# Value panels of the gated feed-forward by seven block products as well

## The chip, the cores and the metric

The kernel runs on one core of a Trainium2 chip. It is one program that does everything from the inputs in the chip's memory to the stored output. The metric is the device time of the launch in microseconds (us). Before the change it is 2545.13 us, the median of three runs (2545.09 to 2545.74).

## The reference

Two transformer blocks of two layers each run over one sequence of 512 tokens with 1024 features. The change touches only the gated feed-forward, which ends both layers of the second block:

```
def swiglu(h, w_in, w_out):
    gu = h @ w_in                       # 1024 x 5632
    gate, up = jnp.split(gu, 2, axis=-1)
    return (jax.nn.silu(gate) * up) @ w_out     # 2816 x 1024
...
x = x + g2 * swiglu(h, ffn_w_in[i], ffn_w_out[i])
```

Everything is in 32-bit floats. The kernel gets that accuracy out of matmuls on rounded numbers: each operand is split into a high part and the rest (low), and a product is low x high, high x low and high x high, three matmuls added up in PSUM.

## The kernel before, in words

**Panels.** Weights come in panels of 128 partitions x 2048 numbers (1 MB). Panel number `at` lies in buffer `at % 2` of three tiles: `RAW` (as loaded), `WH` (high part) and `WL` (low part). SyncE loads a panel into `RAW` as soon as the panel two before it has been split (`split_done`), in the order of the panels. GpSimd (POOL) splits a panel once TensorE has begun the panel before it (`panels_begun`), since only then are `WH` and `WL` of that buffer free. TensorE may begin a panel when it is split.

**One feed-forward** has 11 chunks of 256 hidden features. A chunk has three panels: a gate panel, a value panel (1024 x 256 each) and a down panel (256 x 1024). TensorE's order is: gate of chunk c+1, value of chunk c+1, down of chunk c, gate of chunk c+2, and so on. I call these the stages G, V and D. In D, eight output tiles i = 0..7 go into the banks `DOWN_BANKS`; VectorE (DVE) adds each to the residual `X` (`add`, `residual`, line 3040 of the profile). TensorE waits before tile i for the count of adds `DOWN_FREE[i]`: tile 7 waits until tiles 0 to 3 of this D have been added (bank 1 is used twice).

**Seven block products (`up_fast`).** From chunk 2 on (`FAST_FROM`) the gate panel is multiplied as a 2 x 2 block product with seven half-width products in place of eight (Strassen-Winograd). Each product is 4 x 3 matmuls of 256 columns, 84 in all, where `hidden_t` takes 2 x 8 x 3 = 48 matmuls of 512 columns. The sums that this needs are made beside it:
- `weight_sums`, four DVE operations of 128x512 from `RAW` into `w_sums` (steps 0 to 3); ScalarE (ACT) copies them rounded to `w_sums_hi` (`sums_high`), GpSimd makes `w_sums_lo` (first half of `split_fast`, four operations) and then the low part of the panel (three operations, since one quarter isn't needed); the panel's high part is made by ScalarE (`panel_high`);
- `copy_first` (ACT) copies product 1 within PSUM, and TensorE's product 3 adds to it; `copies` (ACT) take products 2 and 5 out; `combine_first` and `combine` (DVE, four operations of 128x256) add them up. TensorE waits for `copy_first` before product 3 and for `combine_first` before product 5.
- Gate's `up_fast` begins when tiles 0 to 4 of the D before it have been added, and its `copy_first` writes bank 1, so it waits for all eight.

The value panel goes by `hidden_t`, and both it and the down panel are split by GpSimd alone (`split_pieces`: one operation for the high part, four for the low).

**The hidden features** of a chunk: `Silu` of the gate (ACT), times the value (DVE, `u_in`), high part `U` (ACT, `uhi`), low part (DVE, `ulo`), used by the D of the chunk one round later. Each engine's order is written out by hand in its own `swiglu` and `chunk`; within an engine nothing overtakes. DVE's round is: combine the gate, weight sums of the next gate, value times silu, low part, eight adds. The loop takes two chunks a turn; the semaphore counts go by `number`, `fast_at` and `loads`.

Of the kernel before, what the change touches and what calls it, by code (L numbers as in the profile page):

```python
# [26 lines left out]
ALU = mybir.AluOpType  # L27
# [5 lines left out]
KT = D // P  # L33
# [18 lines left out]
DIL = 4  # L52
D_FF2 = 2816
FF2_CHUNKS = D_FF2 // 256
FAST = (0,)
FAST_FROM = 2
FAST_PANELS = len(FAST) * (FF2_CHUNKS - FAST_FROM)
PARTS = 16 * LAYERS + 20
# [10 lines left out]
PN_A = LAYERS * PN_LAYER  # L69
# [364 lines left out]
def build(nc, t, out):  # L434
    with ExitStack() as ctx:
# [478 lines left out]
        def _(pool):  # L914
# [30 lines left out]
            def split_pieces(at):  # L945

                b = at % 2
                pool.wait_ge(raw_ready[b], 16 * loads(at))
                pool.wait_ge(s.panels_begun, at + 2)
                apart(pool)  # L950
                pool.tensor_scalar(WH[b][:, :], RAW[b][:, :], 1.0, 1.0, ALU.mult, ALU.mult).then_inc(s.split_hi, 1)  # L951
                pool.wait_ge(s.split_hi, at + 1)
                for q in range(4):
                    c = slice(S * q, S * q + S)
                    ins = pool.tensor_tensor(WL[b][:, c], RAW[b][:, c], WH[b][:, c].bitcast(F32), ALU.subtract)  # L955
                ins.then_inc(s.split_done, 1)
# [1436 lines left out]
        def _(act):  # L2393
# [388 lines left out]
            def swiglu(w, first, g0, f0, u0):  # L2782

                def number(z, c):

                    return (c - FAST_FROM) * len(FAST) + (FAST_PANELS * w + FAST.index(z))

                def copy_first(z, c):

                    n = number(z, c)  # L2790
                    act.wait_ge(fa.products, fa.products_0 + (n * 5 + 1))
                    if z == 0:
                        act.wait_ge(s.f_evac, c * 8 + (f0 + BANKS - 8))
                    f(PS[:, 3 * z + 1, 0:256], PS[:, 3 * z, 0:256], ACT.Copy).then_inc(fa.copied, 1)

                def copies(z, c):

                    n = number(z, c)
                    act.wait_ge(fa.products, fa.products_0 + (n * 5 + 2))
                    f(p5_copy(z), PS[:, 3 * z + 2, 0:256], ACT.Copy).then_inc(fa.copied, 1)  # L2800
                    act.wait_ge(fa.products, fa.products_0 + (n * 5 + 4))
                    f(p167_copy(z), PS[:, 3 * z + 1, 0:256], ACT.Copy).then_inc(fa.copied, 1)

                def panel_high(z, c, b):

                    act.wait_ge(s.panels_begun, c * 3 + (first + 1 + z))
                    f(WH[b][:, :], RAW[b][:, :], ACT.Copy).then_inc(s.split_hi, 1)

                def sums_high(z, c):

                    if z in FAST:
                        act.wait_ge(fa.sums, fa.sums_0 + ((c - FAST_FROM) * len(FAST) * 4 + ((FAST_PANELS * w + FAST.index(z) + 1) * 4 + 9 * (w + 1))))
                        f(w_sums_hi(z), w_sums(z), ACT.Copy).then_inc(fa.sums_hi, 1)  # L2813

                def chunk(c, e, fast, ahead, normed=False):

                    b0 = (first + e) % 2
                    gate_fast, value_fast = (fast and z in FAST for z in range(2))
                    if value_fast:
                        panel_high(1, c, b0)  # L2820
                    if gate_fast:
                        copy_first(0, c)
                        copies(0, c)
                        act.wait_ge(fa.combined, fa.combined_0 + (number(0, c) * 4 + 4))
                    if value_fast:
                        copy_first(1, c)
                    halves = range(2) if gate_fast else range(1)
                    for j in range(2):
                        act.wait_ge(s.g_tile, c * 4 + (g0 + j + 1))
                        for h in halves:  # L2830
                            src = quarter(0, True, j, h) if gate_fast else PS[:, j, :]
                            dst = SQ[:, j, 256 * h:256 * h + 256] if gate_fast else SQ[:, j, :]
                            ins = f(dst, src, ACT.Silu)
                        ins.then_inc(s.r32, 1)
                    if normed:
                        for x in range(4):
                            act.wait_ge(fa.sums, fa.sums_0 + ((FAST_PANELS * 4 + 9) * w + x + 2))
                            f(h_sums_hi(x), h_sums(x), ACT.Copy).then_inc(fa.sums_hi, 1)
                    if value_fast:
                        copies(1, c)  # L2840
                    if ahead:
                        sums_high(0, c + 1)
                        panel_high(0, c + 1, b0)
                    for j in range(2):
                        if value_fast:
                            act.wait_ge(s.u_in, c * 2 + (u0 + 2))
                            for h in range(2):
                                ins = f(U[:, e, j, 0, 256 * h:256 * h + 256], quarter(1, True, j, h), ACT.Copy)
                            if j:
                                ins.then_inc(s.uhi, 2)  # L2850
                        else:
                            act.wait_ge(s.u_in, c * 2 + (u0 + j + 1))
                            f(U[:, e, j, 0, :], PS[:, 3 + j, :], ACT.Copy).then_inc(s.uhi, 1)
                    if ahead:
                        sums_high(1, c + 1)

                chunk(0, 0, False, False, normed=True)
                chunk(1, 1, False, True)
                with act.Fori(0, (FF2_CHUNKS - 3) // 2) as c2:
                    for e in range(2):  # L2860
                        chunk(c2 * 2 + (2 + e), e, True, True)
                chunk(FF2_CHUNKS - 1, 0, True, False)

            enter(act, ST_A)
            act.dma_start(near, t["dist"][:, D_A:D_A + 3 * P]).then_inc(s.dist_in, 16)
# [132 lines left out]
        def _(dve):  # L2998
# [433 lines left out]
            def swiglu(w, first, g0, f0, u0, gate, norm, add_last=None):  # L3432

                def number(z, c):

                    return (c - FAST_FROM) * len(FAST) + (FAST_PANELS * w + FAST.index(z))
# [56 lines left out]
                        v.wait_ge(fa.sums_hi, fa.sums_hi_0 + ((FAST_PANELS + 4) * w + x + 1))  # L3493
                        v.tensor_tensor(h_sums_lo(x), h_sums(x), h_sums_hi(x).bitcast(F32), ALU.subtract).then_inc(fa.sums, 1)

                def hidden(c, e, fast, ahead=None):

                    gate_fast, value_fast = (fast and z in FAST for z in range(2))
                    if gate_fast:
                        combine_first(0, c)  # L3500
                        combine(0, c)
                    if ahead:
                        weight_sums(0, c + 1, *ahead[0], range(2))
                    if value_fast:
                        combine_first(1, c)
                    if ahead:
                        weight_sums(0, c + 1, *ahead[0], range(2, 4))
                    if value_fast:
                        combine(1, c)
                        v.wait_ge(fa.combined, fa.combined_0 + (number(1, c) * 4 + 4))  # L3510
                    halves = range(2) if value_fast else range(1)
                    for j in range(2):
                        v.wait_ge(s.r32, c * 2 + (u0 - 64 + j + 1))
                        v.wait_ge(s.g_tile, c * 4 + (g0 + 2 + j + 1))
                        for h in halves:
                            x = quarter(1, True, j, h) if len(halves) == 2 else PS[:, 3 + j, :]
                            y = SQ[:, j, 256 * h:256 * h + 256] if len(halves) == 2 else SQ[:, j, :]
                            ins = v.tensor_tensor(x, y, x, ALU.mult)
                        if len(halves) == 1 or j:
                            ins.then_inc(s.u_in, len(halves))  # L3520
                    for j in range(2):
                        v.wait_ge(s.uhi, c * 2 + (u0 + (2 if len(halves) == 2 else j + 1)))
                        for h in halves:
                            x = quarter(1, True, j, h) if len(halves) == 2 else PS[:, 3 + j, :]
                            hi, lo = (U[:, e, j, y, 256 * h:256 * h + 256] if len(halves) == 2 else U[:, e, j, y, :] for y in range(2))
                            ins = v.tensor_tensor(lo, x, hi.bitcast(F32), ALU.subtract)
                        ins.then_inc(s.ulo, 1)
# [4 lines left out]

                def chunk(c, e, fast, ahead):

                    hidden(c + 1, e, fast, ahead)
                    for i in range(4):
                        add(c, range(i, i + 1))
                        if ahead:
                            weight_sums(1, c + 2, *ahead[1], range(i, i + 1))
                    add(c, range(4, KT))  # L3540

                def panel_loaded(c, z, c2=None):

# [163 lines left out]
```

## Time and profile before

| | |
|---|---|
| runs | 2545.09, 2545.13, 2545.74 us |
| profiled execution | 2544.84 us, its span 2543.1 us |
| TensorE | busy 2514.6 us (99%), granted clock 0.999 |
| DVE, ACT, GpSimd | busy 52%, 30%, 56% |
| one round (G, V, D) of the gated feed-forward | 31.86 us |

The span runs from the first instruction to the last; 1.74 us lie around it. Matmuls are pipelined, so that the start of one to the start of the next counts (the pitch), not the duration of one.

### The profile page before, as it was taken

How to read it: one execution, taken by the hardware profiler on the slowest of the kernel's cores; microseconds unless marked ns; L12 is line 12 of the kernel's file. 1: busy time of each engine (PE TensorE's matmuls, PEld its weight loads, DVE VectorE, ACT ScalarE, POOL GpSimd, SP SyncE). 2: the span in 40 equal slices, each digit the busy share in tenths (PEclk: the TensorE clock that was granted, in tenths of full speed). 3: DMA queues.
4: the chain of work that ended last, by engine and by line, in shares of the span. 5: the costliest groups of instructions: out<-in, count | busy, mean ns of one | idle time of the engine just before them, and what ended most of it. 6: DMA issues, size and time to landing. Idle time of an engine off the chain costs nothing. (4 is left out here: it accounts for less than half of the span.)

```text
span 2543.1 us, 37266 instructions
## 1 busy us (share of the span) xinstructions
PE 2514.6 (99%) x15183; PEld 2062.2 (81%) x15183; DVE 1321.6 (52%) x2134; ACT 764.7 (30%) x1483; POOL 1422.2 (56%) x796
## 2 busy tenths in 40 slices
PE   8999999999999999999999999999999999999999
PEld 6787778888887877788888767788888888788888
DVE  4445565666534346656665344655554135755554
ACT  5245451111123454511011443322222333422223
POOL 5543246666565423356655833677776522677776
PEclk9999999999999999999999999999999999999999
DMA  8321034555333211445562211223233211232232
GB/s 268 83 61 51 22 112 149 191 188 185 115 101 83 62 49 34 133 138 181 195 199 100 70 51 36 89 94 99 99 99 126 83 51 35 83 98 99 98 99 71
DMA packets 220459, 265.50 MB, mean 104 GB/s; under 512 B 19236, under 2 KB 192892, under 8 KB 220188
## 3 DMA queue, kind: packets, MB, share of 16 engines
q1 hardware_dynamic: 217628, 256.72, 31.4%
q10 hardware_dynamic: 2688, 6.76, 0.8%
q8 instruction: 104, 1.70, 0.3%
q14 instruction: 39, 0.32, 0.0%
HBM read 258.74 MB, written 4.72 MB: 104 GB/s over the span
## 5 line engine op out<-in xcount | busy, mean ns | idle before, releaser
L923 POOL TENSOR_SCALAR WH<-RAW 128x2048 fp32r<-128x2048 f32 x112 | 215.4, 1924 | 713.3 <-issue 608.7
L925 POOL TENSOR_TENSOR WL<-RAW,WH 128x2048 fp32r<-128x2048 f32 x112 | 519.0, 4634 | 9.3
L1115 PE MATMUL PS<-Hh,WL 128*128 128x512 f32 x864 | 337.3, 390 | 0.7 <-POOL WL L955 0.7
L1118 PE MATMUL PS<-Hl,WH 128*128 128x512 f32 x864 | 336.4, 389 | 0.0
L1119 PE MATMUL PS<-Hh,WH 128*128 128x512 f32 x864 | 336.1, 389 | 0.0
L3040 DVE SCALAR_TENSOR_TENSOR X<-PS,X 128x512 f32<-128x512 f32 x304 | 207.0, 688 | 185.5 <-PE PS L1868 123.3
L955 POOL TENSOR_TENSOR WL<-RAW,WH 128x512 fp32r<-128x512 f32 x192 | 277.7, 1474 | 4.0
L2775 ACT ACTIVATE PS<-SQ 128x512 f32<-128x512 f32 x64 | 38.5, 602 | 557.1 <-DVE SQ L3381 557.1
L1864 PE MATMUL PS<-U,WL 128*128 128x512 f32 x512 | 200.1, 391 | 0.0
L1867 PE MATMUL PS<-U,WH 128*128 128x512 f32 x512 | 199.2, 389 | 0.0
L1868 PE MATMUL PS<-U,WH 128*128 128x512 f32 x512 | 199.2, 389 | 0.0
L1115 PEld LDWEIGHTS PS<-Hh,WL 128*128 128x128 f32 x864 | 162.2, 188 | 35.7 <-POOL WL L955 2.2
L1119 PEld LDWEIGHTS PS<-Hh,WH 128*128 128x128 f32 x864 | 162.2, 188 | 33.9
L1118 PEld LDWEIGHTS PS<-Hl,WH 128*128 128x128 f32 x864 | 162.3, 188 | 32.8
L951 POOL TENSOR_SCALAR WH<-RAW 128x2048 fp32r<-128x2048 f32 x48 | 92.5, 1928 | 162.6 <-issue 162.6
L3040 DVE SCALAR_TENSOR_TENSOR X<-PS,MOD,X 128x512 f32<-128x512 f32 x184 | 132.4, 746 | 64.9 <-PE PS L1986 48.1
L1985 PE MATMUL PS<-U,WH 128*128 128x512 f32 x336 | 130.7, 389 | 0.0
L1986 PE MATMUL PS<-U,WH 128*128 128x512 f32 x336 | 130.7, 389 | 0.0
L1982 PE MATMUL PS<-U,WL 128*128 128x512 f32 x336 | 130.7, 389 | 0.0
L934 POOL TENSOR_TENSOR YL<-DB,YL 128x512 fp32r<-128x512 f32 x72 | 91.0, 1295 | 50.9 <-ACT YL L2813 50.9
L1864 PEld LDWEIGHTS PS<-U,WL 128*128 128x128 f32 x512 | 96.1, 188 | 21.1 <-issue 1.2
L1868 PEld LDWEIGHTS PS<-U,WH 128*128 128x128 f32 x512 | 96.1, 188 | 20.1
(636 smaller groups left out, 5878.6 us busy)
## 6 DMA issues: line engine op xcount, KB each, us to landing
RAW<-in_w_ff SPq DMA_DIRECT2D x64, 1024.0 KB, 5.3
PROJ<-in_ada_w SPq DMA_DIRECT2D x48, 1024.0 KB, 7.9
RAW<-in_ffn_w_in SPq DMA_DIRECT2D x44, 1024.0 KB, 5.1
RAW<-in_ffn_w_out SPq DMA_DIRECT2D x22, 1024.0 KB, 4.9
RAW<-in_w_in SPq DMA_DIRECT2D x20, 1024.0 KB, 5.3
RAW<-in_w_out SPq DMA_DIRECT2D x8, 1024.0 KB, 5.1
RAW<-in_a_w_in SPq DMA_DIRECT2D x6, 1024.0 KB, 5.0
RAW<-in_b_w_in SPq DMA_DIRECT2D x12, 512.0 KB, 5.1
```

What stands on the lines that cost most here:

```text
L923: pool.tensor_scalar(WH[b][:, :], RAW[b][:, :], 1.0, 1.0, ALU.mult, ALU.mult).then_inc(s.split_hi, 1)
L925: pool.tensor_tensor(WL[b][:, :], RAW[b][:, :], WH[b][:, :].bitcast(F32), ALU.subtract).then_inc(s.split_done, 1)
L955: ins = pool.tensor_tensor(WL[b][:, c], RAW[b][:, c], WH[b][:, c].bitcast(F32), ALU.subtract)
L1115: ins = mm(bank, WL[b][:, col:col + P], Hh[:, k, :], start=k == 0, stop=False)
L1118: mm(bank, WH[b][:, col:col + P], Hl[:, k, :], start=False, stop=False)
L1119: ins = mm(bank, WH[b][:, col:col + P], Hh[:, k, :], start=False, stop=k == KT - 1)
L1864: ins = mm(bank, WL[b][:, col:col + P], U[:, c % 2, k, 0, :], start=k == 0, stop=False)
L1867: mm(bank, WH[b][:, col:col + P], U[:, c % 2, k, 1, :], start=False, stop=False)
L1868: ins = mm(bank, WH[b][:, col:col + P], U[:, c % 2, k, 0, :], start=False, stop=k == 1)
L1982: ins = mm(bank, WL[b][:, col:col + P], U[:, e, k, 0, :], start=k == 0, stop=False)
L1985: mm(bank, WH[b][:, col:col + P], U[:, e, k, 1, :], start=False, stop=False)
L3040: v.scalar_tensor_tensor(X[:, tile, :], PS[:, bank, :], gate, X[:, tile, :], ALU.mult, ALU.add).then_inc(evac, 1)
```

## The change

`FAST` becomes `(0, 1)`: the value panels of chunks 2 to 10 go by seven block products as well, 9 in each feed-forward, 18 in all. For them `w_sums` lie in other tiles (`ATT`, `ATTR`, `MEMTR`). With it the order of the helpers moves:
- ACT makes the high part of the value panels (`panel_high(1, ...)`, first thing in G) and of the down panels D(1) to D(9) (`panel_high(2, ...)`, in V ahead of the value's `copy_first`); GpSimd drops that operation in `split_fast` and `split_pieces`. `sums_high(1, ...)` stands before the `U` copies.
- DVE (`hidden`): steps 0 and 1 of the next gate's sums, `combine_first` of the value, steps 2 and 3, `combine` of the value. Then (`between(0)`) the adds of tiles 0 to 3 with the four steps of the next value's sums between them (add 0, steps 0 and 1, add 1, step 2, add 2, step 3, add 3), then value times silu (four of 128x256), adds 4 and 5 (`between(1)`), the low part (four of 128x256), adds 6 and 7.

```diff
--- before.py
+++ after.py
@@ -52,7 +52,7 @@
 DIL = 4
 D_FF2 = 2816
 FF2_CHUNKS = D_FF2 // 256
-FAST = (0,)
+FAST = (0, 1)
 FAST_FROM = 2
 FAST_PANELS = len(FAST) * (FF2_CHUNKS - FAST_FROM)
 PARTS = 16 * LAYERS + 20
@@ -948,7 +948,8 @@
                 pool.wait_ge(raw_ready[b], 16 * loads(at))
                 pool.wait_ge(s.panels_begun, at + 2)
                 apart(pool)
-                pool.tensor_scalar(WH[b][:, :], RAW[b][:, :], 1.0, 1.0, ALU.mult, ALU.mult).then_inc(s.split_hi, 1)
+                if 1 not in FAST or not any(at in range(first + 7, first + 3 * FF2_CHUNKS - 1, 3) for first in (PN_A + 10, PN_B + 11)):
+                    pool.tensor_scalar(WH[b][:, :], RAW[b][:, :], 1.0, 1.0, ALU.mult, ALU.mult).then_inc(s.split_hi, 1)
                 pool.wait_ge(s.split_hi, at + 1)
                 for q in range(4):
                     c = slice(S * q, S * q + S)
@@ -2812,7 +2813,7 @@
                         act.wait_ge(fa.sums, fa.sums_0 + ((c - FAST_FROM) * len(FAST) * 4 + ((FAST_PANELS * w + FAST.index(z) + 1) * 4 + 9 * (w + 1))))
                         f(w_sums_hi(z), w_sums(z), ACT.Copy).then_inc(fa.sums_hi, 1)
 
-                def chunk(c, e, fast, ahead, normed=False):
+                def chunk(c, e, fast, ahead, normed=False, loaded=None):
 
                     b0 = (first + e) % 2
                     gate_fast, value_fast = (fast and z in FAST for z in range(2))
@@ -2823,6 +2824,8 @@
                         copies(0, c)
                         act.wait_ge(fa.combined, fa.combined_0 + (number(0, c) * 4 + 4))
                     if value_fast:
+                        act.wait_ge(raw_ready[1 - b0], loaded)
+                        panel_high(2, c, 1 - b0)
                         copy_first(1, c)
                     halves = range(2) if gate_fast else range(1)
                     for j in range(2):
@@ -2841,6 +2844,7 @@
                     if ahead:
                         sums_high(0, c + 1)
                         panel_high(0, c + 1, b0)
+                        sums_high(1, c + 1)
                     for j in range(2):
                         if value_fast:
                             act.wait_ge(s.u_in, c * 2 + (u0 + 2))
@@ -2851,15 +2855,14 @@
                         else:
                             act.wait_ge(s.u_in, c * 2 + (u0 + j + 1))
                             f(U[:, e, j, 0, :], PS[:, 3 + j, :], ACT.Copy).then_inc(s.uhi, 1)
-                    if ahead:
-                        sums_high(1, c + 1)
-
+
+                down_loads = lambda c: 16 * loads(first + 3 * c + 1)
                 chunk(0, 0, False, False, normed=True)
                 chunk(1, 1, False, True)
                 with act.Fori(0, (FF2_CHUNKS - 3) // 2) as c2:
                     for e in range(2):
-                        chunk(c2 * 2 + (2 + e), e, True, True)
-                chunk(FF2_CHUNKS - 1, 0, True, False)
+                        chunk(c2 * 2 + (2 + e), e, True, True, loaded=c2 * 48 + down_loads(2 + e))
+                chunk(FF2_CHUNKS - 1, 0, True, False, loaded=down_loads(FF2_CHUNKS - 1))
 
             enter(act, ST_A)
             act.dma_start(near, t["dist"][:, D_A:D_A + 3 * P]).then_inc(s.dist_in, 16)
@@ -3493,7 +3496,7 @@
                         v.wait_ge(fa.sums_hi, fa.sums_hi_0 + ((FAST_PANELS + 4) * w + x + 1))
                         v.tensor_tensor(h_sums_lo(x), h_sums(x), h_sums_hi(x).bitcast(F32), ALU.subtract).then_inc(fa.sums, 1)
 
-                def hidden(c, e, fast, ahead=None):
+                def hidden(c, e, fast, ahead=None, between=None):
 
                     gate_fast, value_fast = (fast and z in FAST for z in range(2))
                     if gate_fast:
@@ -3507,6 +3510,9 @@
                         weight_sums(0, c + 1, *ahead[0], range(2, 4))
                     if value_fast:
                         combine(1, c)
+                    if between:
+                        between(0)
+                    if value_fast:
                         v.wait_ge(fa.combined, fa.combined_0 + (number(1, c) * 4 + 4))
                     halves = range(2) if value_fast else range(1)
                     for j in range(2):
@@ -3518,6 +3524,8 @@
                             ins = v.tensor_tensor(x, y, x, ALU.mult)
                         if len(halves) == 1 or j:
                             ins.then_inc(s.u_in, len(halves))
+                    if between:
+                        between(1)
                     for j in range(2):
                         v.wait_ge(s.uhi, c * 2 + (u0 + (2 if len(halves) == 2 else j + 1)))
                         for h in halves:
@@ -3532,12 +3540,18 @@
 
                 def chunk(c, e, fast, ahead):
 
-                    hidden(c + 1, e, fast, ahead)
-                    for i in range(4):
-                        add(c, range(i, i + 1))
-                        if ahead:
-                            weight_sums(1, c + 2, *ahead[1], range(i, i + 1))
-                    add(c, range(4, KT))
+                    def between(x):
+
+                        if x:
+                            add(c, range(4, 6))
+                            return
+                        for i in range(4):
+                            add(c, range(i, i + 1))
+                            if ahead:
+                                weight_sums(1, c + 2, *ahead[1], ((0, 1), (2,), (3,), ())[i])
+
+                    hidden(c + 1, e, fast, ahead, between)
+                    add(c, range(6, KT))
 
                 def panel_loaded(c, z, c2=None):
```

## Rows read from the trace of the kernel before

**Rows 1.** The page, part 1: busy time of TensorE.

```profile
PE 2514.6 (99%) x15183; PEld 2062.2 (81%) x15183; DVE 1321.6 (52%) x2134; ACT 764.7 (30%) x1483; POOL 1422.2 (56%) x796
```

**Rows 2.** Waits of TensorE, 1640 to 1980 us: total, times, longest.

```profile
PE PS L1088 <- ACT Hh L2438: 0.7, 1, 0.7
PE PS L1115 <- POOL WL L955: 0.4, 1, 0.4
```

**Rows 3.** Windows: one round in mid-stage; length, busy time by engine, clock, DMA.

```profile
1759.34:1791.20 31.86, 31.86 (x182) 28.09 (x181) 16.71 (x20) 7.03 (x11) 24.05 (x17) 1.00 0.30 98
```

**Rows 4.** Timeline of TensorE: start, duration; first matmul of G, V, D, G.

```profile
1759.34 0.28 PE L1941 MATMUL PS<-Hh,WL 128*128 128x256 f32 x1
...
1769.41 0.40 PE L1115 MATMUL PS<-Hh,WL 128*128 128x512 f32 x1
...
1780.32 0.39 PE L1982 MATMUL PS<-U,WL 128*128 128x512 f32 x1
...
1791.19 0.28 PE L1941 MATMUL PS<-Hh,WL 128*128 128x256 f32 x1
```

**Rows 5.** Timeline of DVE in that round: start, duration, line, idle before.

```profile
1759.54 0.75 DVE L3040 SCALAR_TENSOR_TENSOR X<-PS,MOD,X 128x512 f32<-128x512 f32 x1 [0.61 <-PE PS L1986]
1763.95 0.42 DVE L3443 TENSOR_TENSOR PTS<-PS,PTS 128x256 f32<-128x256 f32 x1 [3.66 <-PE PS L1945]
...
1769.61 0.43 DVE L3455 TENSOR_TENSOR PS<-RS,PS 128x256 f32<-128x256 f32 x1 [0.92 <-PE PS L1945]
1772.12 1.71 DVE L3467 TENSOR_TENSOR DB<-RAW 128x512 f32<-128x512 f32 x1 [2.08 <-DMA RAW<-in_ffn_w_in]
1773.75 1.77 DVE L3469 TENSOR_TENSOR DB<-RAW 128x512 f32<-128x512 f32 x1
1775.45 1.78 DVE L3472 TENSOR_TENSOR DB<-DB,RAW 128x512 f32<-128x512 f32 x1
...
1784.40 2.72 DVE L3040 SCALAR_TENSOR_TENSOR X<-PS,MOD,X 128x512 f32<-128x512 f32 x4
```

**Rows 6.** Timeline of ACT in that round.

```profile
1761.05 0.37 ACT L2794 ACTIVATE PS<-PS 128x256 f32<-128x256 f32 x1 [9.27 <-PE PS L1945]
...
1770.15 1.21 ACT L2833 ACTIVATE SQ<-PS 128x256 f32<-128x256 f32 x4 [3.04 <-DVE PS L3455]
1778.96 1.92 ACT L2813 ACTIVATE YL<-DB 128x2048 fp32r<-128x2048 f32 x1 [7.59 <-DVE DB L3475]
1780.78 1.90 ACT L2807 ACTIVATE WH<-RAW 128x2048 fp32r<-128x2048 f32 x1
```

**Rows 7.** Timeline of GpSimd in that round.

```profile
1759.80 1.90 POOL L951 TENSOR_SCALAR WH<-RAW 128x2048 fp32r<-128x2048 f32 x1 [1.80 <-issue]
1761.78 5.05 POOL L955 TENSOR_TENSOR WL<-RAW,WH 128x512 fp32r<-128x512 f32 x4
...
1771.99 6.38 POOL L955 TENSOR_TENSOR WL<-RAW,WH 128x512 fp32r<-128x512 f32 x4
1781.05 5.05 POOL L934 TENSOR_TENSOR YL<-DB,YL 128x512 fp32r<-128x512 f32 x4 [2.68 <-ACT YL L2813]
```

**Rows 8.** Timeline of GpSimd in two short windows, where single operations come apart.

```profile
1774.94 3.43 POOL L955 TENSOR_TENSOR WL<-RAW,WH 128x512 fp32r<-128x512 f32 x2
...
1776.64 1.73 POOL L955 TENSOR_TENSOR WL<-RAW,WH 128x512 fp32r<-128x512 f32 x1
```

**Rows 9.** Timeline, ahead of the first D: DVE and then GpSimd.

```profile
1650.51 0.68 DVE L3472 TENSOR_TENSOR DB<-DB,RAW 128x512 f32<-128x512 f32 x1
...
1644.55 5.49 POOL L955 TENSOR_TENSOR WL<-RAW,WH 128x512 fp32r<-128x512 f32 x4
```

**Rows 10.** Timeline of TensorE: first matmul of the first D and of V(2).

```profile
1652.88 0.39 PE L1982 MATMUL PS<-U,WL 128*128 128x512 f32 x1
...
1673.83 0.40 PE L1115 MATMUL PS<-Hh,WL 128*128 128x512 f32 x1
```

**Rows 11.** Timeline, 1024-wide passes: DVE beside GpSimd's splits.

```profile
1623.27 2.32 DVE L3486 TENSOR_TENSOR PROJ<-MEMT,ATT 128x1024 f32<-128x1024 f32 x1
1625.51 2.32 DVE L3488 TENSOR_TENSOR PROJ<-MEMT,PROJ 128x1024 f32<-128x1024 f32 x1
```

## The prediction

> **What bounds the kernel now.** I read the page first: TensorE is busy for 99% of the span [rows 1], so only fewer TensorE cycles or new TensorE idle time can move the end. Then its waits over the nine rounds of the first gated feed-forward: 1.1 us in all, none of it in a fast round [rows 2]. The window of one round says the same: 31.86 us long, TensorE busy for all of it, DVE for 16.71, ACT 7.03, GpSimd 24.05 [rows 3]. TensorE is the bound, with no slack used up; the helpers have room on average. An average doesn't say whether they have it at the right moment, so I laid out one round from the timelines of the four engines [rows 4 to 8].
>
> **The gain.** G is 84 matmuls in 1769.41 - 1759.34 = 10.07 us (pitch 0.120 us), V is 48 in 10.91 us (0.227), D is 48 in 10.87 [rows 4]. Half the columns cost 53% of the time, so seven products in place of eight give little: a fast V should take 10.07, 0.84 less. Times 18 panels: -15.1 us. That is all the change can give.
>
> **Small costs.** GpSimd loses two 1.90 us operations a round [rows 7], gains four of sums_lo (5.05) and drops one low quarter (1.26): it stays at 24 us of about 31. ACT gains three 128x2048 passes of 1.9 and a few small ones: 14 of 31. Their averages are fine; their places matter twice.
> - G: ACT now starts with panel_high(1). It sees G begun 0.46 after the first matmul (as GpSimd at 1759.80 [rows 7]) and takes 1.90, pitch 1.81; copy_first moves from G+1.71 [rows 6] to G+2.27 and ends at +2.64. Product 3's weights load at about G+2.76. I book 0 (bounds 0 and 0.2).
> - V: ACT is held by gate's last combine until V+0.74 (1770.15 [rows 6]); panel_high(2) puts the value's copy_first to 2.55 to 2.92, with product 3 due at 2.88. I book 0.25 a round (bounds 0.1 and 0.5), 4.5 us in all. Silus (pitch 0.27) and product 2's copy follow until V+4.4; combine_first at 4.9 still comes before product 5 wants it at 6.0.
>
> **The price of a weight sum.** A 128x512 sum takes 0.68 us when GpSimd rests [rows 9], and 1.7 us beside GpSimd's low-part operations [rows 5]. The two interlace: GpSimd's operations start at 1774.94 and 1776.64 [rows 8], DVE's at 1773.75 and 1775.45 [rows 5], each pair 1.70 apart. GpSimd's operation alone is 1.26 (5.05 / 4 [rows 7]), so DVE's sum ends some 0.5 after the GpSimd operation that was running, and that engine's next one waits as long. A 1024-wide pass fits: 2.24 from start to start [rows 11], that is 1.26 plus twice the 0.5. DVE's adds, with one input in PSUM, run at 0.66 whether GpSimd is busy or not (2.72 for four [rows 5]). So in a row: a sum ends 0.5 after the current GpSimd operation, and an add between two sums lies under the next GpSimd operation and is nearly free (sum to sum 1.70 to 1.75 with it). The bound on the other side is that it isn't: 1.70 for each sum plus 0.66 for each add.
> The Trainium skill, SBUF — State Buffer, section "SBUF: two separate sides", speaks against this change too: VectorE with two SBUF inputs and GpSimd hold one port pair exclusively, for a whole instruction, and the other blocks. The trace agrees (1.70 against 0.68). By it the adds hide and the sum is the one below; by shared bandwidth it would be the dearer bound.
>
> **The chain that I expect to set the round.** The new value sums can't start before the next value panel is in RAW, and that load waits for the down panel's split in the same buffer, which waits for V to begin. From V's first matmul (0), in the steady state:
> - ACT's panel_high(2) ends at 2.64; GpSimd starts the low part at 2.8 (0.17 later, as from 1780.88 to 1781.05 [rows 6, 7]). Its four operations interlace with three of gate's sums; alone 5.05, so 6.38 as now [rows 7], and DVE's wait for combine_first leaves one gap more: done at 9.35.
> - From there to the first sum: 5.29, as from 1766.83 (1761.78 + 5.05) to 1772.12 [rows 5, 7]. The value's sums start at 14.65. D began at 10.3, tile 0 is long added.
> - GpSimd meanwhile has the next gate panel: sums_high ends at 10.1, so 7 operations from 10.27 (5.05 + 3.8 alone). All four sums meet them: step 0 ends 15.85 (behind GpSimd's fourth), step 1 17.55, add 1 inside, step 2 19.3, step 3 21.0, add 3 21.7.
> - TensorE's tile 7 wants add 3. It was due at 10.3 + 9.5 = 19.8: about 1.9 late. D's last tile ends 23.1.
> - Value times silu: four 256-wide (0.42 each [rows 5], pitch about 0.34): 23.05. Add 4: 23.75; G wants it and starts at 23.9, 0.8 more.
> - Add 5 to 24.4, low part 24.45 to 25.9 (ACT's sums_high(1), 1.9, and U copies end 24.4), adds 6 and 7 to 27.25. Gate's copy_first wants add 7: 27.35 to 27.7; product 3 starts at 27.85 where 26.8 was due: 1.05 more. The other five products take 7.19, and the next V begins at 35.05.
> GpSimd, on the other side, is done with the next value panel at 32.0, and the next gate panel lands at 37.3, 2.25 after V's start, as the layout assumed. The round closes: 35.05 in place of 31.86, +3.2 a round, gain and V's 0.25 included.
>
> **The sum.** Nine rounds from D(0)..D(8) to V(2)..V(10). In the first, D(0) starts at 1652.88 and the panel's split ends at 1650.04 [rows 9, 10]: sums from 1655.3, next V 20.4 later (27.25 - 14.65 + 7.8) at 1675.8 to 1676.3 in place of 1673.83: +2.2. Eight full rounds: 8 x 3.2 = 25.5. The last V: -0.84 + 0.25 = -0.6. Together 27.1, and the second feed-forward alike: +54.2 us. On the profiled execution's 2544.84 us (span 2543.1 and 1.74 around it, 0.3 under the median of 2545.13) that gives 2599.0 us.
>
> **Bounds.** If adds don't hide under GpSimd's operations, three adds cost 0.66 each and the sums begin no earlier: up to 0.95 a round more once the last sum runs partly alone, 2616; with the 256-wide operations at their full 0.43 (0.6 a round over eight, half of it felt) 2622. If two of the four value sums find GpSimd at rest (its seven operations over early), they cost 0.65 for 1.7: about 2 us a round less, +18, 2563. 0.2% (5 us) is about what a measurement of this kernel can tell from no change.
>
> **Rivals.**
> 1. The chain fits and the gain is seen: faster. It needs the value's sums at 0.68 and GpSimd unhindered: the split done at 7.86, sums from 13.15, add 3 at 17.6 with tile 7 due at 19.8, add 7 at about 23.3 with copy_first due at 23.4. The round is then TensorE's 31.02 + 0.25: -15.1 + 4.5 = -10.6, 2534 us. It decides once the chain is under 31.86, 3.2 us shorter than mine. For it: the helpers' averages leave room, and the trace shows sums only beside GpSimd's line 955, where mine meet line 934 too. Against it: the paired starts [rows 5, 8]. 14%.
> 2. The same chain, but DVE pays the full 1.7 for every sum and the adds on top: round 36.0, 2616 us. For it: no row shows an add between two sums. Against: the 1024-wide pass, which splits 2.24 into a wait and its own time. 20%.
> 3. Part of the lateness is absorbed, since a late G gives GpSimd time and it meets fewer sums: a round within 0.3 of 31.86, no measurable change. For it: only the room on average. 4%.
> The forecast as written: 62%. Slower by over 0.2% are the forecast and rival 2, 82%, with rival 3's same at 4% and faster 14%. The range takes in the bounds of the forecast and rival 2, 2563 to 2622; it leaves out rivals 1 and 3 and 2% beyond.
>
> **What the profile after would show.** TensorE's waits: tile 7's first matmul (line 1982 of before) on DVE's add (line 3040), some 1.9 us, 18 times; G's first matmul on the same for 0.8; product 3 of the gate on ACT's copy for 1.0; product 3 of the value for 0.25. Value sums of 1.2 to 1.8 us between the adds, starting some 4.3 after D's first matmul. A round of 35 us, with DVE's idle time gone between there and G. It would be wrong if the sums run at 0.7, if the load comes long before D+4, or if the adds of tiles 0 to 3 end before D+9.5.

## The result: 2594.41 us, 1.9% slower, and the profile after

The changed kernel takes 2594.41 us (median of four runs, 2593.85 to 2596.02), the kernel before 2545.24 on the same chips. The ratio is 1.0194, 95% interval 1.0176 to 1.0212: slower, by 49 us. The forecast was 2599.0 (2563 to 2622). The profiled execution took 2596.02 us with a span of 2594.0, 51.2 above the profiled execution of before; it is the slowest of the four.

The page says first where to look. The row of [rows 1] has become this one, and a TensorE line with idle time in front of it is among the costly groups:

```profile
PE 2520.4 (97%) x15831; PEld 2081.1 (80%) x15831; DVE 1415.1 (55%) x2350; ACT 888.5 (34%) x1627; POOL 1448.9 (56%) x814
...
L1983 PE MATMUL PS<-U,WL 128*128 128x512 f32 x336 | 133.1, 396 | 24.8 <-DVE X L3043 24.8
```

TensorE's share fell from 99% to 97%: it waits. GpSimd's share is the 56% of before, which speaks against its amount of work as the cause (one of the experiments tests it). TensorE's waits over the whole span (total, times, longest), where [rows 2] had nothing:

```profile
PE PS L1983 <- DVE X L3043: 24.8, 18, 1.7
...
PE PS L1942 <- ACT PS L2795: 8.1, 17, 0.7
PE PS L1942 <- DVE X L3043: 8.0, 17, 0.5
```

Line 1983 is the first matmul of a down tile and waits for an add 18 times (tile 7); line 1942 (first matmul of each step of a half-width product) waits for an add at the start of G and for ACT's copy ahead of product 3. The windows of one round, stage by stage (G, V, D; the columns are those of [rows 3]):

```profile
1805.30:1816.19 10.89, 10.43 (x84) 10.23 (x85) 4.42 (x10) 3.34 (x6) 8.04 (x7) 1.00 0.22 78
1816.19:1826.54 10.35, 10.33 (x87) 10.13 (x85) 6.96 (x8) 5.88 (x9) 6.66 (x4) 1.00 0.18 62
1826.54:1840.19 13.65, 11.41 (x51) 8.69 (x49) 10.43 (x15) 4.69 (x6) 10.89 (x8) 1.00 0.40 125
```

V did get shorter, 10.35 for 10.91. D grew from 10.87 to 13.65 and G from 10.07 to 10.89. A round is 34.87 us (278.96 from V(2) to V(10), over 8) in place of 31.86; the first two are longer, 35.14 and 35.32, since TensorE waits there for `combine_first` ahead of the value's product 5 (0.54 and 1.77 us), and the other six are 34.75 on average. DVE's timeline in D and the next G shows why a round is long:

```profile
1830.94 1.28 DVE L3470 TENSOR_TENSOR ATT<-RAW 128x512 f32<-128x512 f32 x1 [2.06 <-DMA RAW<-in_ffn_w_in]
1832.15 1.77 DVE L3472 TENSOR_TENSOR ATT<-RAW 128x512 f32<-128x512 f32 x1
1833.85 0.74 DVE L3043 SCALAR_TENSOR_TENSOR X<-PS,MOD,X 128x512 f32<-128x512 f32 x1
1834.51 1.12 DVE L3475 TENSOR_TENSOR ATT<-ATT,RAW 128x512 f32<-128x512 f32 x1
1835.55 0.74 DVE L3043 SCALAR_TENSOR_TENSOR X<-PS,MOD,X 128x512 f32<-128x512 f32 x1
1836.21 1.10 DVE L3478 TENSOR_TENSOR ATT<-RAW,ATT 128x512 f32<-128x512 f32 x1
1837.24 0.74 DVE L3043 SCALAR_TENSOR_TENSOR X<-PS,MOD,X 128x512 f32<-128x512 f32 x1
1837.90 1.41 DVE L3524 TENSOR_TENSOR PS<-SQ,PS 128x256 f32<-128x256 f32 x4
1839.22 1.40 DVE L3043 SCALAR_TENSOR_TENSOR X<-PS,MOD,X 128x512 f32<-128x512 f32 x2
1840.59 1.42 DVE L3534 TENSOR_TENSOR U<-PS,U 128x256 fp32r<-128x256 f32 x4
1841.93 1.40 DVE L3043 SCALAR_TENSOR_TENSOR X<-PS,MOD,X 128x512 f32<-128x512 f32 x2
```

The row at 1830.94 waits for the load of the next value panel; behind it DVE has not a moment's rest until 1843.33, and the adds that TensorE wants stand in that queue. From one sum to the next, with an add between them, it is 1.70 us (1834.51 to 1836.21), as long as sum to sum without one ([rows 5]). The load waits for GpSimd's split of the down panel, which waits for ACT, and ACT for DVE's last combine of the gate, 0.6 us after V's start at 1816.19:

```profile
1817.01 1.92 ACT L2808 ACTIVATE WH<-RAW 128x2048 fp32r<-128x2048 f32 x1 [3.11 <-DVE PS L3458]
```

```profile
1819.01 6.66 POOL L956 TENSOR_TENSOR WL<-RAW,WH 128x512 fp32r<-128x512 f32 x4 [5.67 <-ACT WH L2808]
```

GpSimd sat idle for 5.67 us before it. And TensorE, in the D and G one round ahead of those rows of DVE, at tile 7 (1803.15), at G (1805.30) and at gate's product 3 (1808.89); a round later the three waits are 1.74, 0.50 and 0.46:

```profile
1803.15 0.50 PE L1983 MATMUL PS<-U,WL 128*128 128x512 f32 x1 [1.60 <-DVE X L3043]
...
1805.30 0.38 PE L1942 MATMUL PS<-Hh,WL 128*128 128x256 f32 x1 [0.50 <-DVE X L3043]
...
1808.89 0.39 PE L1942 MATMUL PS<-PROJR,YL 128*128 128x256 f32 x1 [0.46 <-ACT PS L2795]
```

### The profile page after: what moved, and what is told of

Read it like the earlier page. It is cut to its first block and busy times, and to the rows that moved or that the text cites. A ratio compares the mean times of both kernels' runs of the same rounds, so it can differ in the third digit from the quotient of the medians.

```text
span 2594.0 us, 39234 instructions
## 1 busy us (share of the span) xinstructions
PE 2520.4 (97%) x15831; PEld 2081.1 (80%) x15831; DVE 1415.1 (55%) x2350; ACT 888.5 (34%) x1627; POOL 1448.9 (56%) x814
## 3 DMA queue, kind: packets, MB, share of 16 engines
q8 instruction: 106, 1.74, 0.3%
## 5 line engine op out<-in xcount | busy, mean ns | idle before, releaser
L923 POOL TENSOR_SCALAR WH<-RAW 128x2048 fp32r<-128x2048 f32 x112 | 215.8, 1926 | 713.4 <-issue 594.4
L956 POOL TENSOR_TENSOR WL<-RAW,WH 128x512 fp32r<-128x512 f32 x120 | 188.3, 1599 | 100.7 <-ACT WH L2808 99.7
L1116 PE MATMUL PS<-Hh,WL 128*128 128x512 f32 x576 | 225.0, 391 | 0.8 <-POOL WL L956 0.8
L1119 PE MATMUL PS<-Hl,WH 128*128 128x512 f32 x576 | 224.1, 389 | 0.0
L1120 PE MATMUL PS<-Hh,WH 128*128 128x512 f32 x576 | 224.1, 389 | 0.0
L1116 PEld LDWEIGHTS PS<-Hh,WL 128*128 128x128 f32 x576 | 108.1, 188 | 24.7 <-POOL WL L956 2.2
L2808 ACT ACTIVATE WH<-RAW 128x2048 fp32r<-128x2048 f32 x54 | 103.6, 1918 | 67.3 <-DVE PS L3458 55.7
L1120 PEld LDWEIGHTS PS<-Hh,WH 128*128 128x128 f32 x576 | 108.1, 188 | 22.7
L1119 PEld LDWEIGHTS PS<-Hl,WH 128*128 128x128 f32 x576 | 108.1, 188 | 22.2
L934 POOL TENSOR_TENSOR ATTR<-ATT,MEMTR 128x512 fp32r<-128x512 f32 x72 | 90.6, 1290 | 39.0 <-ACT MEMTR L2814 39.0
```

Source lines behind the costliest of these rows:

```text
L1116: ins = mm(bank, WL[b][:, col:col + P], Hh[:, k, :], start=k == 0, stop=False)
L1119: mm(bank, WH[b][:, col:col + P], Hl[:, k, :], start=False, stop=False)
L1120: ins = mm(bank, WH[b][:, col:col + P], Hh[:, k, :], start=False, stop=k == KT - 1)
```

## The experiments

Ten kernels ran; "round" is a steady one, from one V to the next in the middle of the first feed-forward. The first two rounds are longer in some kernels, so that the mean of the eight lies above it: 31.77 for 31.68 with the memsets, 33.24 for 32.94 with the narrow operations, 33.59 for 33.49 with half the load. Each was timed against the kernel before on its chip (2544.97 to 2545.35). "Sums" are the value's weight sums unless said otherwise.

### Only the moves

```diff
-FAST = (0, 1)
+FAST = (0,)
...
-                    if value_fast:
+                    if gate_fast:
                         act.wait_ge(raw_ready[1 - b0], loaded)
                         panel_high(2, c, 1 - b0)
-                        copy_first(1, c)
```

> Only the moves: the value panels go by the 48 matmuls of before, but ACT makes the high part of the down panels at V's start, and DVE keeps the new places of the adds, the product with the silu and the low part. Theory 1 (the loss comes from the value's sums on the chain from V to gate's copy_first): nothing on that chain is left, every round 31.86 us, 2545 us within 3. Rival A (the moves themselves make TensorE wait, ACT's extra 1.9 us or DVE's adds before the product): rounds over 33 us, above 2565 us.

Measured: 2545.03 us, ratio 1.000 (0.999 to 1.001). TensorE's waits in the first feed-forward are those of [rows 2] again. This kernel leaves the value's seven products out, and with them ACT's high part of the value panels, and keeps the other moves (GpSimd still drops the down panels' high part). These moves alone cost nothing; the loss is the value's seven products and what they need.

### The sums made cheap

```diff
-v.tensor_tensor(y[0], part(1, 0), part(1, 1), ALU.add).then_inc(fa.sums, 1)
+(v.memset(y[0], 1.0) if z else v.tensor_tensor(y[0], part(1, 0), part(1, 1), ALU.add)).then_inc(fa.sums, 1)
```

(and so for the other three)

> The changed kernel with the value's four weight sums replaced by four memsets of the same 128x512 regions by DVE: the value's sums are left out of the computation, everything that waits for them stays. Theory 1 (each sum costs 1.7 us because DVE and GpSimd take turns): a memset reads nothing, so about 0.6 us each; add 3 at 19.0 us after V's start, tile 7 on time, add 7 at 24.6, gate's copy_first still some 1.2 us late: round 32.2 to 32.5 in place of 34.9, so 2550 to 2556 us in place of 2594. Rival B (the wait for the load alone, or TensorE's 256-column matmuls, make the loss): the round stays over 34 us, 2585 or more.

Measured: 2543.88 us (ratio 0.9995, 0.9986 to 1.0005), round 31.68. All 50 us are gone, more than I expected: add 3 was done 18.6 us after V's start (I had written 19.0) and add 7 after 23.9 (24.6), since a memset with the add behind it took 1.09 where I had put down 1.26, and the 256-wide operations less than I had booked. DVE and then GpSimd:

```profile
1816.49 0.48 DVE L3470 MEMSET ATT<- 128x512 f32 x1 [2.16 <-DMA RAW<-in_ffn_w_in]
1817.04 0.48 DVE L3472 MEMSET ATT<- 128x512 f32 x1
```

```profile
1817.08 1.29 POOL L939 TENSOR_TENSOR WL<-RAW,WH 128x512 fp32r<-128x512 f32 x1
1818.33 2.55 POOL L942 TENSOR_TENSOR WL<-RAW,WH 128x512 fp32r<-128x512 f32 x2
```

A memset of the same region beside GpSimd is 0.48 long, and GpSimd's operations keep their 1.27. The sums' price is the loss. But even with almost free sums there is no gain over the kernel before: G is 10.42 and V 10.35 where 10.08 each would be enough. Both of ACT's copies (`copy_first`) still come late, the value's right behind a 2048-wide pass, the gate's because it waits for add 7:

```profile
1825.61 0.37 ACT L2795 ACTIVATE PS<-PS 128x256 f32<-128x256 f32 x1 [0.47 <-DVE X L3043]
```

### GpSimd's part of the price

```diff
-first = lambda x: x[:, 0:1024].rearrange("p (k i c) -> p k i c", k=4, i=2)[:, :, 0, :]
+first = lambda x: x[:, 0:1024].rearrange("p (k i c) -> p k i c", k=4, i=2)[:, :, 0, 0:(P if z else 16)]
...
-                    c = slice(S * q, S * q + S)
+                    c = slice(S * q, S * q + (S if z else 64))
```

> The changed kernel with GpSimd's three low-part operations of the gate panels (lines 939 and 942) cut to an eighth of their width: most of the gate weights' low part is left out, DVE's work is untouched. Theory 1 (DVE's sums are long only beside a full GpSimd operation): steps 1, 2 and 3 of the value's sums fall from 1.7 to about 0.65 us, tile 7 is on time, round about 33.0, 2560 to 2566 us. Rival B (DVE's sums are long for their own sake, by their strided reads of RAW): no DVE operation changes, round 34.9, 2594 us.

Measured: 2566.12 us, round 32.94, as theory 1 has it (the time is at the upper edge of what I wrote). DVE's code is unchanged, but its steps beside the narrowed operations fell from 1.77 (step 1) and 1.12 (step 2) to 0.81 and 0.68, what a sum takes alone:

```profile
1825.22 0.81 DVE L3472 TENSOR_TENSOR ATT<-RAW 128x512 f32<-128x512 f32 x1
1825.95 0.74 DVE L3043 SCALAR_TENSOR_TENSOR X<-PS,MOD,X 128x512 f32<-128x512 f32 x1
1826.61 0.68 DVE L3475 TENSOR_TENSOR ATT<-ATT,RAW 128x512 f32<-128x512 f32 x1
```

So the length of the sums is GpSimd's doing and not that of their strided reads. This speaks with the run before it for one mechanism: DVE's sums, with two inputs in SBUF, take turns with GpSimd's operations; the adds, with one input in PSUM, and the memsets don't. The Trainium skill, SBUF — State Buffer, section "Who interferes with whom", says of trn2 that a DVE operation with two SBUF inputs contends with a GpSimd operation that reads SBUF, and that one with at most one SBUF input (outside the modes that use both ports) doesn't. The traces agree: 1.70 us a turn, adds and memsets unhindered.

### The load in the chain

```diff
-                    panel(b, at, KT, 256, t["ffn_w_in_2"][l, :, bass.ds(f0, 256)])
...
+                    if half:
+                        panel(b, at, 4, 256, t["ffn_w_in_2"][l, 0:512, bass.ds(f0, 256)])
+                    else:
+                        panel(b, at, KT, 256, t["ffn_w_in_2"][l, :, bass.ds(f0, 256)])
```

(`half` is set for the value panels of the loop)

> The changed kernel with only the first half (512 KB) of each value panel loaded: half of the value weights are stale, all operations stay. Theory 1 (the load of the next value panel is on the chain, 5.3 us from the down panel's split to the first sum): the sums start some 2.3 us earlier and the whole chain with them, round about 32.6, 2552 to 2558 us. Rival C (GpSimd's 25 us of work or DVE's own total sets the round): the load is hidden, round 34.9, 2594 us.

Measured: 2574.61 us, round 33.49, between theory 1 and the rival: the load is on the chain, but I had its share too large. The sum starts 3.69 us after the split's end (5.27 with the full load), not 3, and DVE's first sum met more of GpSimd's work (1.63 for 1.28):

```profile
1813.13 6.50 POOL L959 TENSOR_TENSOR WL<-RAW,WH 128x512 fp32r<-128x512 f32 x4 [5.67 <-ACT WH L2811]
```

```profile
1823.32 1.63 DVE L3473 TENSOR_TENSOR ATT<-RAW 128x512 f32<-128x512 f32 x1 [0.31 <-DMA RAW<-in_ffn_w_in]
```

### The down panel's high part back on GpSimd

```diff
-                        act.wait_ge(raw_ready[1 - b0], loaded)
-                        panel_high(2, c, 1 - b0)
```

(with GpSimd's operation for all down panels again)

> The changed kernel with one part undone: GpSimd makes the high part of the down panels D(1) to D(9) again, ACT doesn't. Theory 1 (the chain runs through the split of the down panel, and GpSimd has idle time ahead of it): GpSimd begins the split at V+0.46 in place of waiting for ACT until V+2.8, is done with the high part at 2.4 and with the low part some 0.4 us earlier than now; the value's copy_first is on time too. The round gets 0.2 to 0.4 us shorter or stays as it is, 2587 to 2594 us. Rival (GpSimd's amount of work is the bound, which the move to ACT relieved): 1.9 us more in each round, 2620 to 2628 us.

Measured: 2594.90 us, mean of the eight rounds 34.77 (34.87 in the changed kernel), the same as the changed kernel within its scatter, a little above the upper edge of what I wrote. GpSimd starts its four low-part operations 0.4 us earlier, counted from V's start, and ends them only 0.16 earlier (6.86 us for the four in place of 6.66). The rival, GpSimd's amount of work, is out: 1.9 us more of it in a round cost nothing. The move of this operation to ACT, a part of the change, is worth nothing here.

### DVE's order

```diff
-                    if between:
-                        between(0)
...
+                        for x in [0, 'm', 's01', 1, 's2', 2, 's3', 3, 4, 5, 6, 7, 'l']:
+                            if x == "m":
+                                times()
+                            elif x == "l":
+                                low()
+                            elif isinstance(x, int):
+                                add(c, range(x, x + 1))
+                            elif ahead:
+                                weight_sums(1, c + 2, *ahead[1], tuple(int(y) for y in x[1:]))
...
-                        sums_high(1, c + 1)
                     for j in range(2):
...
+                    if ahead:
+                        sums_high(1, c + 1)
```

Numbers are adds, `m` is value times silu, `sN` steps of the sums, `l` the low part.

> The changed kernel with DVE's order after add 0 altered: value times silu at once (into the idle time before the load lands), then sums and adds as they were, then adds 4 to 7, low part last; ACT's U copies before sums_high of the value. No operation is added or left out. Theory 1: add 3 stays where it is, so tile 7's wait of 1.6 us stays; add 4 and add 7 come 1.4 and 2.8 us earlier, so G's first matmul and gate's product 3 wait no more: round about 33.7, 2570 to 2576 us. Rival (GpSimd's chain from sums_high of the value to the split of the value panel sets the round): no shorter than now, 2594 us.

Measured: 2581.48 us, round 33.64. The round is what I expected, the time is 5 us more. TensorE's waits in this kernel:

```profile
PE PS L1983 <- DVE X L3044: 19.7, 18, 1.2
...
PE PS L1942 <- DVE PTS L3447: 8.8, 16, 0.6
```

The waits at G and at gate's product 3 are gone, as expected, and tile 7's has stayed, at 1.1 us on average (1.4 in the changed kernel). What came up in their place is the value's product 5, which waits 0.6 for combine_first behind gate's first two sums. I had also overlooked the end: with the low part last, D(10), which has no G and V ahead of it, waits 2.2 us for it in each feed-forward. The next two kernels have that wait too.

### The lessons put together

```diff
-                        for x in [0, 'm', 's01', 1, 's2', 2, 's3', 3, 4, 5, 6, 7, 'l']:
+                        for x in [0, 'm', 1, 's01', 2, 3, 's2', 4, 5, 's3', 6, 7, 'l']:
...
+                    if z:
+                        act.wait_ge(fa.sums, fa.sums_0 + ((c - FAST_FROM) * len(FAST) * 4 + ((FAST_PANELS * w + FAST.index(z) + 1) * 4 - 1 + 9 * (w + 1))))
+                        f(odd_even(w_sums_hi(z), 0), odd_even(w_sums(z), 0), ACT.Copy).then_inc(s.sums_half, 1)
...
+                    pool.wait_ge(s.sums_half, n // 2 + 1)
+                    for q in (0, 2):
```

(The first pair of lines is against the order of the run before, the rest against the changed kernel.) The second half of the value's sums_high follows after step 3, and GpSimd's quarters 1 and 3 after that. Besides, DVE makes the value's combine_first ahead of gate's four sums, ACT makes gate's copy_first ahead of the value's panel_high, and the down panel's high part is GpSimd's.

> The whole of the computation, with the lessons put together: the down panel's high part by GpSimd; DVE makes the value's combine_first ahead of gate's four sums, then after add 0 value times silu, add 1, steps 0 and 1, adds 2 and 3, step 2, adds 4 and 5, step 3, adds 6 and 7, low part; ACT makes gate's copy_first ahead of the value's panel_high, U copies ahead of sums_high, and the value's sums_high in two halves, the first after step 2, so that GpSimd can begin their low part earlier. Theory 1: tile 7, G and both product 3s are on time, GpSimd is done with the value panel about 0.2 to 1 us ahead of V: round 31.05 to 31.5 us, 2531 to 2540 us, faster than both kernels. Rival (GpSimd's 27 us with the turns it takes with DVE come too late for V): round 31.9 to 33, 2545 to 2565 us, with TensorE waiting for GpSimd at V's start.

> As e7_reordered, but the value's sums_high in one piece after step 3. Theory 1: GpSimd begins the low part of the value's sums 2 to 2.5 us later and ends about 0.7 us behind V's due start: round 31.7 to 32.2, 2542 to 2551 us, TensorE waiting for GpSimd at the start of V. Rival (GpSimd has room): same as e7_reordered.

Measured: 2559.57 us, round 32.41, with the halves; 2586.94 us, round 33.79, without. Both missed what I expected of theory 1. The first lies in the range of its rival, whose cause (GpSimd too late) is the right one, though it put the wait at V. TensorE's waits, with the halves and then without:

```profile
PE PS L1951 <- POOL WL L951: 16.1, 16, 1.1
```

```profile
PE PS L1942 <- POOL WL L942: 34.9, 32, 1.3
```

All waits for DVE and ACT in the rounds had gone, but GpSimd was late, at G (where I had not looked) and, without the halves, at V as well. The layout had let gate's sums slide to 4.97 us after V's start, behind combine_first, and so gate's sums_high (1814.57, with V at 1804.70) and GpSimd's work behind it:

```profile
1814.57 1.92 ACT L2828 ACTIVATE YL<-DB 128x2048 fp32r<-128x2048 f32 x1 [2.08 <-DVE DB L3492]
```

```profile
1816.67 5.96 POOL L943 TENSOR_TENSOR YL<-DB,YL 128x512 fp32r<-128x512 f32 x4 [4.00 <-ACT YL L2828]
```

So there is a second chain, GpSimd's: a split, the load behind it, sums, their high part, the next split. It was hidden under DVE's.

### Gate's sums in halves too, and the last order

The first kernel halves gate's sums_high as well and puts the low part ahead of the last chunk's adds; the second also takes this order:

```diff
-[0, 'm', 1, 's01', 2, 3, 's2', 4, 5, 's3', 6, 7, 'l']
+[0, 'm', 's01', 1, 2, 3, 's2', 4, 's3', 5, 6, 7, 'l']
```

> As e7_reordered (round 32.40 us, of which G waits 1.1 for GpSimd's split of the gate panel), with gate's sums_high in two halves too, the first after step 2, and the low part ahead of the last chunk's adds (D(10) waited 2.2 us for it in each feed-forward). Theory 1: GpSimd begins gate's low parts 1.6 us earlier, G is on time, gate's product 3 waits 0.5 for add 7: round 31.3 to 31.8, 2535 to 2546 us. Rival (the wait moves on to tile 7, product 3 or V by as much): round over 32.2, 2551 us or more.

> As e9_halves_both, with DVE's order steps 0 and 1, adds 1, 2 and 3, step 2, add 4, step 3, adds 5, 6 and 7. Theory 1: step 3 meets GpSimd one operation earlier and add 7 ends 0.6 to 0.9 us earlier, in time for gate's copy_first: round 31.1 to 31.4, 2531 to 2540 us, below the kernel before (2545). Rival (the halves leave the turns of DVE and GpSimd as they are): as e9_halves_both or longer.

Measured: 2540.42 us (ratio 0.9982, 0.9973 to 0.9991), round 31.69; and 2530.63 us (0.9945, 0.9932 to 0.9959), round 31.06, just under the range I gave. In the first, TensorE still waits 0.4 us in a round, at G for an add (and not at gate's product 3, as I had expected). The last kernel is 14.3 us faster than the kernel before, nearly all of the 15.1 that the prediction had as the most the change can give. A window of it as long as a round (31.06, and 0.04 more), and three rows of DVE:

```profile
1796.55:1827.65 31.10, 31.10 (x218) 29.21 (x218) 20.61 (x32) 12.20 (x20) 26.75 (x20) 1.00 0.30 101
```

```profile
1811.71 1.07 DVE L3481 TENSOR_TENSOR ATT<-RAW 128x512 f32<-128x512 f32 x1
1812.71 1.78 DVE L3483 TENSOR_TENSOR ATT<-RAW 128x512 f32<-128x512 f32 x1
1814.41 2.06 DVE L3054 SCALAR_TENSOR_TENSOR X<-PS,MOD,X 128x512 f32<-128x512 f32 x3
```

TensorE has no wait left in the rounds. The value's sums are hardly shorter than in the changed kernel (5.03 us for the four, 5.27 there), and GpSimd is busy for longer in a round than there (26.75 us for 25.58). They have only been moved to where nobody waits.

## Why the prediction was right, point by point

- **The bound and the gain.** Right: TensorE set the round, and the fast V takes 10.07 to 10.09 us where nothing delays it (three of the reordered kernels). With the chain out of the way the whole gain comes out.
- **The chain.** Right in each link. After V's start: the split's end 9.48 (9.35 forecast), first sum 14.75 (14.65), add 3 done 21.8 (21.7), add 4 done about 23.7 (23.75), add 7 done 27.14 (27.25), next V 34.89 (35.05). Changing DVE's order alone gave back 13 us of the 49, shortening the load alone 20, sparing three of the four sums GpSimd's turns 28, and the memsets all of it; the moves without the value's products lost nothing.
- **The turns.** Right, and it decided between the forecast and rival 2: sum, add, sum takes 1.70 us, so the add lies under GpSimd's operation. Had it been on top, the round would have been 36.
- **Waits of TensorE.** Right in place and nearly in size. The prediction priced by how much later TensorE starts; the idle time in the profile is shorter than that. D takes 2.78 longer in the round shown and 2.6 on average of the six later ones (forecast 2.7): tile 7 starts 1.8 to 2.0 late (1.9), with 1.6 to 1.74 of it idle, and G 0.8 (0.8), with 0.5 idle. The value's product 3 made V 0.28 longer than 10.07 (0.25). Gate's product 3 was booked too dear: G is 0.82 longer (1.05). G began 0.1 later than forecast, add 7 was done 0.1 earlier (the two groups of four 256-wide operations took 1.32 and 1.34 where 1.35 and 1.45 were booked), and from add 7 to TensorE's start behind the copy it was 0.45 in place of 0.60.
- **The sum.** D(10) of the first feed-forward starts 25.9 us later than before: 2.5 up to V(2) (2.2 forecast; 0.65 of it was there already at D(0), for which nothing was booked), eight rounds of 3.01 (3.2), last V -0.7 (-0.6). The second gives 25.0, and the span is 50.9 longer; 54.2 was forecast. The mean of 3.01 hides two errors of opposite sign. The six later rounds are 2.9 longer than before. The first two are 3.3 and 3.5 longer, by the wait for `combine_first` ahead of the value's product 5. The prediction had it in time (4.9 us after V's start, with 6.0 due); in V(3) it was done after 7.9, behind gate's first sums, which began 5.0 us after V's start there (2.5 in the round shown). At 2.9 for all eight, each feed-forward would have come out 1 us lower: that much of the nearness is luck. The forecast of 2599.0 is 3.0 above the profiled execution and 4.6 above the median.
- **The rivals.** Rival 1 would have needed sums without GpSimd's turns. The memset kernel comes nearest to that case, though gate's sums keep their turns there and the split ends at 9.45 us after V's start, where the rival had 7.86. Its 2543.88 speaks for my 2534 being too low: add 7 is done at 23.9 (23.3 in the rival), and gate's product 3, for which I had booked nothing, makes G 0.35 longer. Rival 3's absorption didn't come.
- **What I didn't see.** The loss was a matter of order, and the same work in another order wins. The prediction looked for what sets the round and found DVE's chain. It has GpSimd done with the value panel at 32.0 (measured 32.03), 3 us ahead of the next V, but takes that for room and doesn't say that it hangs on a chain of its own, which the first reordered kernels ran into.

## What to carry to other kernels

Before a helper engine gets work in each round of a loop that TensorE bounds, lay out the helpers' round with the loads in it: a buffer that is split, reloaded and summed closes a chain that can be longer than the round while no helper is busy for more than three quarters of it (GpSimd 25.58 of 34.89 us here). Price DVE operations with two SBUF inputs beside a busy GpSimd by turns (here GpSimd's 1.26 plus 0.44 us for 128x512), and put work with an input in PSUM between them, which was free here. When the round is late, first try to move work that nobody waits for (here the product and the low part) out from behind a late load, and hand a long pass over in halves; look for the second chain before the first is gone.

## What the runs showed of the hardware that I had not expected

- Half the load (512 KB for 1024) came 3.69 us after the split in place of 5.27: 1.6 us less for half the bytes.
- GpSimd's operations at 64 columns (an eighth) still took 0.5 us (1.05 for two), for 1.27 at full width.
- A sum that meets one of GpSimd's operations doesn't always take 1.7 us: in the changed kernel the first of gate's sums starts 0.3 us ahead of GpSimd's first operation on the down panel (1818.70 and 1819.01), takes 0.69, and GpSimd's operation takes 1.54 in place of 1.26.
